# Norm weights read from one small tile through TensorE, a new order in gating with the output projection, and the z projection in halves of 264 columns

## The reference

```python
def rms_norm(x, g, eps=EPS):
    y = xf * lax.rsqrt(jnp.mean(xf * xf, -1, keepdims=True) + eps)
    return (y * g.astype(jnp.float32)).astype(x.dtype)
# layer 0
h = rms_norm(x, p['norm_mix_pre'][layer])
cols = h @ p['w_in_even'][i]                 # z: 512 columns, a and b: 16 columns, and q, k, v, RWKV
o = rms_norm(o_fwd + o_bwd, o_norm) * jax.nn.silu(z)        # gdn, o_norm has 128 weights for each head
y = ((y - mean) * lax.rsqrt(var + RWKV_LN_EPS)) * ln_g + ln_b;  y = (y + bonus) * gate     # rwkv
mix = jnp.concatenate([a_out, b_out], -1) @ p['w_out_even'][i]
x = x + rms_norm(mix, p['norm_mix_post'][layer])            # then the norm before the MLP
```

## Time and profile before

| | us |
|---|---|
| median of 3 runs (lowest, highest) | 4776.31 (4774.74, 4781.5) |
| the profiled execution | 4772.9 |
| its span, first to last instruction | 4771.1 |
| PE busy over the span | 4243.3 (89%) |
| mean granted clock of PE, share of full | 0.924 |

### The profile page before, as it was taken

One profiled execution on the slowest core, in us unless ns is written; L12 is line 12 of the kernel. 1 busy time (PEld: TensorE's weight loads), 2 busy tenths in 40 slices (PEclk: granted clock), 3 DMA queues, 4 the chain that ended last, 5 costly groups with the idle time before them and its releaser, 6 DMA issues. The chain is left out here.

```text
span 4771.1 us, 62898 instructions
## 1 busy us (share of the span) xinstructions
PE 4243.3 (89%) x24064; PEld 3646.5 (76%) x24064; DVE 2215.6 (46%) x3168; ACT 1398.3 (29%) x2254; POOL 1169.7 (25%) x658
## 2 busy tenths in 40 slices
PE   7898886989998999687999999879998879999996
PEld 5777665888888888566888888667886668888885
DVE  4633053555555555654344433456663244433343
ACT  3211064333333333223111111234543321111111
POOL 1111033333333333323111111113331121111112
PEclk8999776999999999797999999879999889999998
DMA  3132176111111111213111111120001121111112
GB/s 95 69 91 75 54 259 235 44 49 47 50 45 45 45 45 36 78 56 115 35 35 44 35 35 44 34 84 10 7 1 40 59 83 38 41 35 44 35 35 88
DMA packets 204867, 285.99 MB, mean 60 GB/s; under 512 B 31096, under 2 KB 148088, under 8 KB 204688
## 3 DMA queue, kind: packets, MB, share of 16 engines
q1 hardware_dynamic: 204688, 283.40, 18.2%
HBM read 205.37 MB, written 77.99 MB: 59 GB/s over the span
## 5 line engine op out<-in xcount | busy, mean ns | idle before, releaser
L592 DVE TENSOR_TENSOR top_acc<-top_acc,ffn_bank 128x512 f32<-128x512 f32 x640 | 440.0, 687 | 399.9 <-PE ffn_bank L109 399.9
L107 PE MATMUL ffn_bank<-hT_ffn_high,ffn_w_high 128*128 128x512 f32 (+1 forms) x1536 | 544.9, 355 | 28.9 <-DVE ffn_w_low L569 28.9
L108 PE MATMUL ffn_bank<-hT_ffn_low,ffn_w_high 128*128 128x512 f32 (+1 forms) x1536 | 544.6, 355 | 0.0
L109 PE MATMUL ffn_bank<-hT_ffn_high,ffn_w_low 128*128 128x512 f32 (+1 forms) x1536 | 544.5, 354 | 0.0
L107 PE MATMUL ffn_bank<-ffn_w_high,ffn_f_high 128*128 128x512 f32 x1280 | 498.3, 389 | 0.0
L108 PE MATMUL ffn_bank<-ffn_w_low,ffn_f_high 128*128 128x512 f32 x1280 | 498.3, 389 | 0.0
L109 PE MATMUL ffn_bank<-ffn_w_high,ffn_f_low 128*128 128x512 f32 x1280 | 497.9, 389 | 0.0
L584 DVE TENSOR_TENSOR ffn_square<-ffn_relu 128x512 f32<-128x512 f32 (+1 forms) x192 | 146.7, 764 | 661.8 <-ACT ffn_relu L537 661.8
L107 PEld LDWEIGHTS ffn_bank<-hT_ffn_high,ffn_w_high 128*128 128x128 f32 x1536 | 291.3, 190 | 71.0 <-issue 29.7
L108 PEld LDWEIGHTS ffn_bank<-hT_ffn_low,ffn_w_high 128*128 128x128 f32 x1536 | 291.3, 190 | 41.5
L109 PEld LDWEIGHTS ffn_bank<-hT_ffn_high,ffn_w_low 128*128 128x128 f32 x1536 | 291.2, 190 | 40.3
(11 more groups left out here) (422 smaller groups left out, 9515.5 us busy)
## 6 DMA issues: line engine op xcount, KB each, us to landing
ffn_w_raw<-in_w_ff SPq DMA_DIRECT2D x64, 1024.0 KB, 5.4
s_x<-top_acc SPq DMA_DIRECT2D x30, 512.0 KB, 5.1
norm_x_old<-s_x SPq DMA_DIRECT2D x30, 512.0 KB, 4.5
s_tm_both<-prepare_tb SPq DMA_DIRECT2D x20, 512.0 KB, 7.4
s_fm_dir<-prepare_fd SPq DMA_DIRECT2D x20, 512.0 KB, 6.6
scan_tb<-s_tm_both SPq DMA_DIRECT2D x20, 512.0 KB, 3.5
scan_fb<-s_fm_both SPq DMA_DIRECT2D x20, 512.0 KB, 4.3
scan_fd<-s_fm_dir SPq DMA_DIRECT2D x20, 512.0 KB, 6.2
```

The lines of the kernel that those rows point to most:

```text
L107: pe.matmul(out, stationary[0], moving[0], start=start, stop=False)
L108: pe.matmul(out, stationary[0], moving[1], start=False, stop=False)
L109: return pe.matmul(out, stationary[1], moving[0], start=False, stop=stop)
L592: dve.tensor_tensor(a, a, bank[4 + u % 4][:, :], ALU.add).then_inc(added, 1)
```

## The change

1. **Gains.** One tile `gain_rows` of 64 partitions by 128 holds all four norm weights of both layers, eight rows for each, loaded by four DMAs behind the identity at the kernel's start. `gain(name, layer)` gives the first row. For each gain PE does eight fp32 matmuls of 128 columns: the stationary operand is one column of the identity, repeated 128 times by a step of 0, which picks one row of `gain_rows` and puts it on all partitions. The rows' loads, the ones and their waits go. DVE waits for the first gain only, and for all of them at t = -1, ahead of `mixer(1)`.
2. **z projection.** The 528 columns are cut into two halves of 264. ACT applies SiLU to 264 columns of the first bank and 248 of the second, DVE copies the last 16 and multiplies z by `o_norm`, which is loaded here; SP stores z after this.
3. **Gating and projection.** `o_norm` is gone from POOL (two products for each tile); all eight weight splits are on DVE; load(0) goes ahead of `ln_g` and `ln_b`; DVE waits for these only ahead of `normalize(0)`; `high(0)` on ACT and `low(0)` on DVE stand amid the weight splits; PE's `turn(t + 1)` stands between the two halves of tile t; DVE does `low(t + 1)` between sums and normalize of t + 2.

```diff
@@ -45,6 +45,7 @@
...
+NORM_WEIGHTS = ("norm_mix_pre", "norm_mix_post", "norm_ffn_pre", "norm_ffn_post")
@@ -114,7 +115,7 @@
...
-def residual_norm(nc, E, x_src, x_dst, hT, ident, X, g_post, g_pre):
+def residual_norm(nc, E, x_src, x_dst, hT, ident, gain_rows, X, g_post, g_pre):
@@ -124,7 +125,6 @@
...
-    gain_row, one_row = E.sb("gain_row", [1, len(gain_in), D]), E.sb("one_row", [1, P])
@@ -132,9 +132,9 @@
...
-    (row_loaded, one_set, gains, eps_set, mix_squares, mix_root, mix_inverse, mix_scaled, x_updated, x_squares, x_root, x_inverse, h_ready,
+    (gains, eps_set, mix_squares, mix_root, mix_inverse, mix_scaled, x_updated, x_squares, x_root, x_inverse, h_ready,
...
-        E.sem(n) for n in ("row_loaded", "one_set", "gains", "eps_set", "mix_squares", "mix_root", "mix_inverse", "mix_scaled", "x_updated",
+        E.sem(n) for n in ("gains", "eps_set", "mix_squares", "mix_root", "mix_inverse", "mix_scaled", "x_updated",
@@ -156,8 +156,6 @@
...
-            for i, g in enumerate(gain_in):
-                sp.dma_start(gain_row[:, i, :], g.unsqueeze(0)).then_inc(row_loaded, 16)
@@ -205,7 +203,6 @@
...
-            pool.memset(one_row[:, :], 1.0).then_inc(one_set, 1)
@@ -233,8 +230,10 @@
...
-            dve.wait_ge(gains, len(gain_in))
+            dve.wait_ge(gains, 1)
...
+                if t == -1:
+                    dve.wait_ge(gains, len(gain_in))
@@ -244,12 +243,11 @@
...
-            pe.wait_ge(one_set, 1)
-            pe.wait_ge(row_loaded, 16 * len(gain_in))
-            for i in range(len(gain_in)):
-                for half in range(2):
-                    at = slice(half * 512, (half + 1) * 512)
-                    last = pe.matmul(gain_ps[i][:, at], one_row[:, :], gain_row[:, i, at], start=True, stop=True)
+            n_rows = gain_rows.shape[0]
+            for i, first in enumerate(gain_in):
+                for k in range(KB):
+                    row = ident[0:n_rows, first + k:first + k + 1].broadcast_to([n_rows, P])
+                    last = pe.matmul(gain_ps[i][:, k * P:(k + 1) * P], row, gain_rows[:, :], start=True, stop=True)
@@ -398,22 +396,26 @@
...
-def in_proj_tm(nc, E, hT, w_in, gates, z_dst):
+def in_proj_tm(nc, E, hT, w_in, gates, o_norm_w, z_dst):
...
+    H = (GW + n_ab) // 2
+    REST = GW - H
...
+    o_norm = E.sb("o_norm", [P, GD])
...
-    w_loaded, w_high, w_low, multiplied, silu_done, ab_done = (
-        E.sem(n) for n in ("w_loaded", "w_high", "w_low", "multiplied", "silu_done", "ab_done"))
+    w_loaded, o_norm_loaded, w_high, w_low, multiplied, silu_done, z_done, ab_done = (
+        E.sem(n) for n in ("w_loaded", "o_norm_loaded", "w_high", "w_low", "multiplied", "silu_done", "z_done", "ab_done"))
...
+            sp.dma_start(o_norm[:, :], o_norm_w.partition_broadcast(P)).then_inc(o_norm_loaded, 16)
...
-                sp.wait_ge(silu_done, t + 1)
+                sp.wait_ge(z_done, t + 1)
@@ -422,15 +424,15 @@
...
-                    pe.wait_ge(silu_done, t - 3)
+                    pe.wait_ge(silu_done, 2 * (t - 3))
...
-                for half, (c0, n) in enumerate(((0, GW), (GW, n_ab))):
+                for half in range(2):
...
-                        last = product(pe, bank[2 * (t % 4) + half][:, 0:n], both(hT, slice(None), k, slice(t * P, (t + 1) * P)),
-                                       both(w, slice(None), k, slice(c0, c0 + n)), k == 0, k == KB - 1)
-                last.then_inc(multiplied, 1)
+                        last = product(pe, bank[2 * (t % 4) + half][:, 0:H], both(hT, slice(None), k, slice(t * P, (t + 1) * P)),
+                                       both(w, slice(None), k, slice(half * H, (half + 1) * H)), k == 0, k == KB - 1)
+                    last.then_inc(multiplied, 1)
@@ -438,20 +440,26 @@
...
-                act.wait_ge(multiplied, t + 1)
+                act.wait_ge(multiplied, 2 * t + 1)
...
-                act.activation(z[t % 2][:, :], bank[2 * (t % 4)][:, :], ACT.Silu).then_inc(silu_done, 1)
+                act.activation(z[t % 2][:, 0:H], bank[2 * (t % 4)][:, 0:H], ACT.Silu).then_inc(silu_done, 1)
+                act.wait_ge(multiplied, 2 * t + 2)
+                act.activation(z[t % 2][:, H:GW], bank[2 * (t % 4) + 1][:, 0:REST], ACT.Silu).then_inc(silu_done, 1)
...
+            dve.wait_ge(o_norm_loaded, 16)
...
-                dve.wait_ge(multiplied, t + 1)
-                dve.tensor_copy(gates[:, t, :], bank[2 * (t % 4) + 1][:, 0:n_ab]).then_inc(ab_done, 1)
+                dve.wait_ge(silu_done, 2 * t + 2)
+                dve.tensor_copy(gates[:, t, :], bank[2 * (t % 4) + 1][:, REST:H]).then_inc(ab_done, 1)
+                zh = z[t % 2][:, :].rearrange("p (h n) -> p h n", n=GD)
+                dve.tensor_tensor(zh, zh, bcm(o_norm[:, :], GH), ALU.mult).then_inc(z_done, 1)
...
+            dve.wait_ge(z_done, TILES)
@@ -1931,8 +1939,7 @@
...
-    ON_POOL = KB // 2
-    o_norm = E.sb("o_norm", [P, GD])
+    FIRST = 3
@@ -1947,8 +1954,8 @@
...
-    w_high, w_low_dve, w_low_pool, turned, high_done, low_done, multiplied, done = (
-        E.sem(n) for n in ("w_high", "w_low_dve", "w_low_pool", "turned", "high_done", "low_done", "multiplied", "done"))
+    w_high, w_low, turned, high_done, low_done, multiplied, done = (
+        E.sem(n) for n in ("w_high", "w_low", "turned", "high_done", "low_done", "multiplied", "done"))
@@ -1969,10 +1976,9 @@
...
-            sp.dma_start(o_norm[:, :], ins["gdn_o_norm"][0].partition_broadcast(P)).then_inc(params, 16)
+            load(0)
...
-            load(0)
@@ -1995,20 +2001,17 @@

             turn(0)
             for t in range(TILES):
-                if t + 1 < TILES:
-                    turn(t + 1)
                 pe.wait_ge(low_done, t + 1)
                 if t >= 2:
                     pe.wait_ge(done, t - 1)
                 for half in range(2):
                     for k in range(KB):
                         if t + half == 0:
-                            if k < ON_POOL:
-                                pe.wait_ge(w_low_dve, k + 1)
-                            else:
-                                pe.wait_ge(w_low_pool, k - ON_POOL + 1)
+                            pe.wait_ge(w_low, k + 1)
                         last = product(pe, ps[2 + t % 2][:, half, :], both(mT[t % 2], slice(None), k),
                                        both(w, slice(None), k, slice(half * 512, (half + 1) * 512)), k == 0, k == KB - 1)
+                    if half == 0 and t + 1 < TILES:
+                        turn(t + 1)
                 last.then_inc(multiplied, 1)

         @block.scalar
@@ -2038,14 +2041,15 @@

             act.wait_ge(eps_set, 2)
             square(0)
+            square(1)
             root(0)
-            square(1)
             for k in range(KB):
+                if k == FIRST + 1:
+                    high(0)
                 if k % PER == 0:
                     act.wait_ge(w_loaded[k // PER], 16)
                 act.activation(w[0][:, k, :], w_raw[:, k, :], ACT.Copy).then_inc(w_high, 1)
             root(1)
-            high(0)
             for t in range(TILES):
                 if t + 2 < TILES:
                     square(t + 2)
@@ -2064,15 +2068,9 @@
...
-                link(pool.tensor_tensor(og, og, bcm(o_norm[:, :], GH), ALU.mult))
...
-            pool.wait_ge(params, 48)
-            scale(0)
-            for k in range(ON_POOL, KB):
-                pool.wait_ge(w_high, k + 1)
-                pool.tensor_tensor(w[1][:, k, :], w_raw[:, k, :], w[0][:, k, :].bitcast(F32), ALU.subtract).then_inc(w_low_pool, 1)
-            for t in range(1, TILES):
+            for t in range(TILES):
@@ -2114,24 +2112,26 @@

             dve.memset(eps_g[:, :], EPS).then_inc(eps_set, 1)
             dve.memset(eps_r[:, :], LN_EPS).then_inc(eps_set, 1)
-            dve.wait_ge(params, 48)
             centre(0)
             centre(1)
             sums(0)
+            dve.wait_ge(params, 32)
             normalize(0)
-            for k in range(ON_POOL):
+            for k in range(KB):
+                if k == FIRST:
+                    low(0)
                 dve.wait_ge(w_high, k + 1)
-                dve.tensor_tensor(w[1][:, k, :], w_raw[:, k, :], w[0][:, k, :].bitcast(F32), ALU.subtract).then_inc(w_low_dve, 1)
+                dve.tensor_tensor(w[1][:, k, :], w_raw[:, k, :], w[0][:, k, :].bitcast(F32), ALU.subtract).then_inc(w_low, 1)
             sums(1)
             normalize(1)
-            low(0)
             for t in range(TILES):
                 if t + 2 < TILES:
                     centre(t + 2)
                     sums(t + 2)
-                    normalize(t + 2)
                 if t + 1 < TILES:
                     low(t + 1)
+                if t + 2 < TILES:
+                    normalize(t + 2)
             dve.wait_ge(used_r, TILES)


@@ -2914,12 +2914,20 @@
...
+        gain_rows = top.sb("gain_rows", [2 * KB * len(NORM_WEIGHTS), P])
+
+        def gain(name, layer):
+            return KB * (2 * NORM_WEIGHTS.index(name) + layer)
+
...
```

(17 more changed lines are left out.)

## The result

The changed kernel takes **4704.6 us** (median of four executions, 4699.55 to 4713.73) where the kernel before takes 4776.41 (four executions on the same chip, 4774.74 to 4781.5). The ratio is 0.985, with a 95% interval of 0.983 to 0.987: 71.8 us less. The forecast was 4706 in a range of 4694 to 4722. The profiled execution took 4699.55 us, its span is 4697.5 (before 4771.1), the mean granted clock 0.932 (before 0.924).

A forecast was written before the change was run, and what follows sets the result against it. The prediction took TensorE (PE), busy 89% of the span, as the bound. Its terms -33.8, -22.5 and -13.5 sum to -69.8 us, from 4776.3 to 4706 us, range 4694 to 4722.

The forecast's parts named there:

- Part 1: z projection: 480 matmuls of 264 columns replace the 512 and 16 column ones, with `o_norm` applied there; -33.8 us.
- the 256-column row: Trace row of 256-column matmuls 0.12 us apart at full clock, from which a 264-column one was priced at 0.1233 us.
- The price of the thin ones: z projection before: each 16-column matmul takes 0.117 us at the full clock, put down to the weight load.
- The rival of a clock that still drops: z projection: PE's clock still falls despite the halves, so the kernel takes 4716 to 4729 us; chance 0.10.
- 264 columns that leave the fast rate: z projection: 264 fp32r columns cost more than 256, up to 4858 us, slower than before; chance 0.01.
- some 75 us instead of 109: Sign for the z projection: how long the stage should last after the change, against before.
- Part 2: Norm stages and kernel start: gains from one small tile, DVE starts earlier in norm1 to norm4; -22.5 us.
- the rival wanted 0.4: Norms: the broadcast column loads slowly, gain passes lie 0.4 us apart, norms give nothing, kernel 4731 us; chance 0.08.
- I take off 0.4 in each of three stages: norm1 to norm3: mixer(1) waits for the second gain, so POOL's second add is late; 0.4 us lost in each.
- The later start of norm0: Kernel start: four gain-row loads behind the identity on SP make norm0's first tile 1.5 us late.
- Part 3: Gating stage: new order, first tile written at 2000.3 instead of 2014.4, steady state gaining nothing; -13.5 us, between -8 and -17.
- its last sign: Gating: the prediction is wrong if PE waits in the middle of tile 0 beyond 31 us into the stage.

The follow-up runs named there:

- e4_interleave: Kernel before, z projection with the same matmuls but three of 512 columns and three of 16 taking turns; 4770.11 us, ratio 0.9982.
- e1_halves: Kernel before with only the z projection cut into halves of 264 columns, `o_norm` left in the gating stage; 4742.51 us, ratio 0.9921.
- e10_both_gains: Changed kernel, but DVE waits for both gains at the start of the norm, ahead of mixer(0); 4711.27 us.
- e11_both_moves: Changed kernel, DVE's wait for the second gain moved behind mixer(1), and in gating low(t+1) put behind normalize(t+2); 4707.51 us.
- e6_low_last: Changed kernel, but in the gating stage DVE does low(t+1) behind normalize(t+2) again; 4709.4 us.

## Why the prediction was right

**Part 1 (-33.8, measured -33.4).** Each step held. About 20 matmuls were cold (0.22 us apart from 478.2 to 482.5), the clock rose 4.4 us in and stayed at 1.00, and the rest took 0.122 us each against 0.1233 from the 256-column row. The gap rule of the Trainium skill for isolated matmuls (TensorE: Matmul & The Clock Gate, Back-to-back issue gap), 0.1125 us, would have put the stage 4 to 5 us lower; the measurement sides with the row. The price of the thin ones was right (`e4_interleave`: 0.116). What was wrong is a reason: "They are also the one thing in this stage during which the array streams little, and I put the lower clock down to them too.". The thin ones ran at the full clock, the drops came in the wide ones behind each block of 24, and in turns of three they no longer went with a drop. Taking them away was enough for the sum, but the drops hang on how they follow each other, and why stays open. The rival of a clock that still drops is refuted, 264 columns that leave the fast rate as well.

Where the 33.4 us come from can now be said: the z stage before had seven of its tiles at 9.8 instead of 8.24, which cost 11 us; ten tiles at 5.85 instead of 8.23 are 23.8; together 34.8, and `e1_halves`, which has nothing else, measured 34.4. In the whole change the product by `o_norm` at the end of the last tile takes 1.0 of it back. The "some 75 us instead of 109" among the signs fits no cut by stages (67.6 instead of 101.0); the difference does.

**Part 2 (-22.5, measured -27.7).** The mechanism was right and the size too small. Of "the first gain is there 3.85 us into the stage" the profile shows 3.76 in norm1 and norm3; the second came at 7.17 (`e10_both_gains`), not 7.3. The broadcast column costs nothing, 32 passes take 7.16 us, 0.22 each, where the rival wanted 0.4. Three terms were mis-sized:
- norm2 and norm4 were costed cold. PE comes warm into both: 16 passes take 2.19 us in norm4 (the 0.12 of the earlier trace rows was the right row), and DVE starts 2.7 and 2.2 us in. norm2 gave 8.4 instead of 6.85. norm4 gave 4.8 instead of 3.8; DVE's start gave 5.4, and 0.6 of that did not reach the end. `x_old`, named as next late, is the likely reason, but norm4 took 34.0 to 35.3 us in the kernels with this code, so a difference of 0.6 is not shown.
- "I take off 0.4 in each of three stages" for POOL's late second add: nothing of it is left at the end of the stage. `e11_both_moves`, rightly read, and norm1 (DVE's start 6.9 earlier, stage 7.0 shorter) both say 0. In norm3 DVE's start came 7.4 earlier and the stage is 7.9 shorter; the 0.5 left over is open.
- The later start of norm0, 1.5 us: its own start moved by 1.4 (3.23 to 4.67), but the z projection behind it starts only 0.5 later.

**Part 3 (-13.5, measured -14.5).** The head was followed almost step by step: splits done 23.7 us into the stage (23.5 by the prediction), turn(1) at 31.3 (31.1), first write at 39.3 (39.5). `normalize(0)` came at 8.0 instead of 7.2. By the letter of its last sign the prediction would be wrong, since PE waits in tile 0 beyond 31 us; its own working had 31.1, so the sign was set too tight. Three experiments, each taking one thing out of the change, account for most of the 14.3 us of the head: 3.7 for `centre` ahead of the wait for `ln_b`, 5.5 for the half of tile 0 ahead of turn(1), 1.6 for the splits off POOL; some 3.5 were not tried by themselves. Steady state: 12.5 us by the prediction, 12.33 to 12.38 in most tiles of the profile, and the nine tiles 108.4 instead of 109.0. That `low` ahead of `normalize` is what holds the tile at this pace is shown by `e6_low_last` (11.79 without it).

**Sum.** By its own rows the sum is off by a few tenths (11.05 - 3.85 is 7.2, 7.5 - 3.85 is 3.65, -14.1 + 0.5 is -13.6), which changes nothing. Part 1 gave 0.4 us less than its term, parts 2 and 3 gave 5.2 and 1.0 more, and the untouched stages were 2.0 longer in this pair of profiles: the span fell by 73.6 where the sum had 69.8. By the medians the change gives 71.8. That the median came within 1.4 us of the forecast is in part luck: it lies 5.0 us above the profiled execution of the kernel after, and 3.5 above that of the kernel before.

## What to carry to other kernels

Where each matmul loads new weights, share out the columns of a product evenly over them: matmuls of 16, 128, 256 and 264 columns took 0.116, 0.110, 0.120 and 0.122 us here, so 512 + 16 pays for 16 columns nearly what 264 cost, and 264 + 264 pays nothing for it. Read an engine's clock by stretches and not by the mean of the span, and when a short stage gets faster in one run look whether the clock of its first microseconds changed before the edit gets the credit; a second profile of the same code (here the gating stage of two kernels, first writes 1.8 us apart) says how much that is. In a stage where two engines are nearly balanced, ask of each reordering not only what pace it gives but what it costs once to change over; over ten tiles the one-time stall (3.7 and 5.8 us) ate the better pace (0.4 to 0.6 a tile).
